# One transformer-trunk layer on one core: five 1024-column gate products as seven-product block sums, attention steps gathered among the transposed products

## The reference

```
h = rmsnorm(x, ln_g)
qa, ka, va, za, qb, ckv, iq, ik, iw, zb, qc, kc, vc, zc, ga, gb, gc = split(h @ w_in)   # 2048 rows deep
ya = mixer_a(qa, ka, va) * silu(za)       # window of two chunks, sinks, T5 bias
yb = mixer_b(qb, ckv, iq, ik, iw) * silu(zb)   # top-64 keys of an indexer, latent keys and values
yc = mixer_c(qc, kc, vc) * silu(zc)       # chunk-causal, relative bias
merged = sigmoid(ga) * (ya @ w_pa) + sigmoid(gb) * (yb @ w_pb) + sigmoid(gc) * (yc @ w_pc)
out = rmsnorm(x + merged @ w_o, final_g)
```

## Time and profile before

| | |
|---|---|
| median of three runs | 973.84 us |
| the profiled execution's own time | 973.51 us |
| its span, first to last instruction | 971.6 us |
| PE busy | 961.6 us (99%), 5114 matmuls |
| DVE busy | 608.5 us (63%) |
| ACT busy | 473.0 us (49%) |
| POOL busy | 28.2 us (3%) |
| DMA queues of SP | 56.9% of the 16 engines |
| granted PE clock | 0.997 of full speed |

### The profile page before, as it was taken

The page is one execution under the profiler, slowest core; times in us unless marked ns, Lnnn a source line. Parts: engine busy times, 40 slices in busy tenths (PEclk is TensorE's granted clock), DMA queues, the critical chain, the costliest instruction groups (busy, mean ns, idle before and its releaser), DMA issues.

```text
span 971.6 us, 13291 instructions
## 1 busy us (share of the span) xinstructions
PE 961.6 (99%) x5114; PEld 813.1 (84%) x5114; DVE 608.5 (63%) x1135; ACT 473.0 (49%) x786; POOL 28.2 (3%) x26
## 2 busy tenths in 40 slices
PE   9999999999999999999999999999999999999996
PEld 8788888888888888888888888888888888888885
DVE  7585755777675776586765655766655555555553
ACT  6564544555454545454453545544534443444442
POOL 0030000000000110010000000000000000000000
PEclk9999999999999999999999999999999999999998
DMA  8754755464653755564654745646555576555553
GB/s 342 274 194 130 244 200 187 151 225 162 207 205 120 253 174 180 189 207 157 222 199 139 261 157 178 227 149 216 167 193 179 191 304 221 186 184 187 174 177 126
DMA packets 54766, 190.34 MB, mean 196 GB/s; under 512 B 6192, under 2 KB 7088, under 8 KB 54064
## 3 DMA queue, kind: packets, MB, share of 16 engines
q1 hardware_dynamic: 54416, 189.23, 56.9%
q10 hardware_dynamic: 288, 0.27, 0.1%
HBM read 187.38 MB, written 2.10 MB: 195 GB/s over the span
## 4 chain that ended last, share of the span: by engine, by line
PE 94%; DVE 2%; DMA 2%; issue 1%; ACT 0%; SPq 0%; POOLq 0%; POOL 0%; DVEq 0%; ACTq 0%
PE bank L1025 23%; PE bank L1006 18%; PE bank L1008 18%; PE bank L1007 18%; PE bank L1028 12%; PE bank L981 2%; PE bank L1061 2%; PE bank L1081 2%; DMA raw<-in_w_s_dram 2%; DVE w_lo L626 1%; DVE hT L693 0%; ACT w_hi L444 0%; PE bank L1198 0%; DVE scores L686 0%; DVE denom L678 0%
## 5 line engine op out<-in xcount | busy, mean ns | idle before, releaser
L626 DVE TENSOR_TENSOR w_lo<-raw,w_hi 128x1024 fp32r<-128x1024 f32 (+2 forms) x326 | 387.2, 1211 | 172.8 <-ACT w_hi L444 171.4
L444 ACT ACTIVATE w_hi<-raw 128x1024 fp32r<-128x1024 f32 (+2 forms) x326 | 334.8, 1046 | 297.0 <-PE bank L1008 204.0
L1025 PE MATMUL bank<-hT,w_hi 128*128 128x512 f32 x976 | 306.2, 397 | 0.0
L1008 PE MATMUL bank<-w_hi,hT 128*128 128x512 f32 x568 | 221.1, 389 | 0.0
L1028 PEld LDWEIGHTS bank<-hT,w_lo 128*128 128x128 f32 x976 | 181.1, 188 | 41.1
L1006 PE MATMUL bank<-w_hi,hT 128*128 128x512 f32 x504 | 197.2, 391 | 0.0
L1007 PE MATMUL bank<-w_lo,hT 128*128 128x512 f32 x504 | 196.1, 389 | 0.0
L1028 PE MATMUL bank<-hT,w_lo 128*128 128x256 f32 x976 | 190.8, 278 | 0.0
L1025 PEld LDWEIGHTS bank<-hT,w_hi 128*128 128x128 f32 x976 | 150.6, 189 | 3.9
L1008 PEld LDWEIGHTS bank<-w_hi,hT 128*128 128x128 f32 x568 | 106.6, 188 | 22.3
L1006 PEld LDWEIGHTS bank<-w_hi,hT 128*128 128x128 f32 x504 | 94.6, 188 | 20.4 <-issue 0.2
(11 more groups left out here) (149 smaller groups left out, 559.6 us busy)
## 6 DMA issues: line engine op xcount, KB each, us to landing
raw<-in_w_s_dram SPq DMA_DIRECT2D x314, 512.0 KB, 4.4
bias_t<-in_bias_dram SPq DMA_DIRECT2D x24, 384.0 KB, 3.1
raw<-in_w_s_dram SPq DMA_DIRECT2D x6, 456.0 KB, 5.7
merged<-in_x_dram SPq DMA_DIRECT2D x2, 1024.0 KB, 10.5
raw<-in_w_s_dram SPq DMA_DIRECT2D x8, 256.0 KB, 3.1
big<-in_x_dram SPq DMA_DIRECT2D x1, 2048.0 KB, 9.8
out_dram<-big SPq DMA_DIRECT2D x8, 256.0 KB, 2.6
big<-in_x_t_dram SPq DMA_DIRECT2D x7, 256.0 KB, 5.9
```

The source lines that it names most:

```text
L444: nc.scalar.activation(halves(g)[0], raw[:, s, 0:n], ACT.Copy).then_inc(hi_ready, 1)
L626: nc.vector.tensor_tensor(low, raw[:, s, 0:n], high.bitcast(F32), ALU.subtract).then_inc(lo_ready, 1)
L1008: ins = mm(acc, xl, wh[:, e, :], start=False, stop=kt == n_kt - 1)
L1025: mm(bank[2 * (c % 2) + n][:, :], wh[:, e, n * P:(n + 1) * P], hl_t[:, kt, :, :], start=kt == 0, stop=False)
```

## The change

Five of the six gate parts of 1024 columns become one chunk of kind `G` (the first part, `ga`'s left half, stays as two `g` chunks). A `G` chunk takes the 2048-deep product as eight pairs of depth tiles, `k` and `k + 8`. In four of the eight pairs (`S` in `GROUPS`) the 2 x 2 block product (two halves of depth, two of rows; two of depth, two of columns) is formed with seven block products in place of eight. The other four pairs (`p`) are plain. An `S` pair has four pieces, whose block products are 2, 1, 2 and 2 (each is three matmuls of 512 columns); its first two come from DRAM, the last two are sums of weight blocks that POOL writes into `usum` (a ring of two). A `p` pair has two pieces of four block products.

ACT and DVE split the summed pieces like all others. The sums of activation blocks are made once, in chunks `g(0,0)` to `g(0,1)`. `G` accumulates in seven banks besides bank 7 for the plain part, so no attention may be under way: all 25 slots move ahead into the `q`, `k` and `z` chunks. There, slots up to 6 are five pieces apart and those behind alternate between five and two. The exponentials and the normalisation each come one step sooner after their scores. `z(0)` moves behind `k`, so attention output is now copied out by ACT unmultiplied (four copies a slot pair) and multiplied by `silu` at the end of each `z` chunk. The selection rounds of mixer B move from `z(0)` to the `q` chunks. `raw` gets six slots.

```diff
+GROUPS = "SpSpSpSp"
 def branch(b):
-    return [k for n in range(4) for k in (("g", b, n), ("P", b, n))]
+    first = [("g", b, 0), ("P", b, 0), ("g", b, 1), ("P", b, 1)]
+    return ((first if b == 0 else [("G", b, 0), ("P", b, 0), ("P", b, 1)])
+            + [("G", b, 1), ("P", b, 2), ("P", b, 3)])
+def group_pieces():
+    summed, plain = iter(range(NS)), iter(range(NS, 8))
+    return [(part, i) for k in GROUPS for i in [next(summed if k == "S" else plain)]
+            for part in (("11 22", "21 12", "U1 U3", "U2 U4") if k == "S" else ("p 11 22", "p 21 12"))]
...
-          + quarters("k", 0) + quarters("z", 1)
-          + branch(0) + quarters("z", 2) + branch(1) + branch(2) + quarters("o", 0))
+          + quarters("k", 0) + quarters("z", 0) + quarters("z", 1) + quarters("z", 2)
+          + branch(0) + branch(1) + branch(2) + quarters("o", 0))
+RAWS = 6
...
 def slots():
-    yield -1, FIRST[AT["z", 0, 3]]
-    whole = [g for g in range(FIRST[AT["q", 1, 0]], END["k", 0, 3]) if KIND_OF[g] in "qk"]
-    for i in range(8):
-        yield i, whole[2 + 6 * i]
-    for b in range(2):
-        yield 8 * b + 8, FIRST[AT["z", b + 1, 0]] + 2
-        for k in range(7):
-            yield 8 * b + 9 + k, FIRST[AT["g", b, 0]] + 2 + 6 * k
+    for i in range(-1, 7):
+        yield i, FIRST[AT["q", 1, 0]] + 2 + 5 * (i + 1)
+    for i in range(7, 24):
+        yield i, FIRST[AT["k", 0, 0]] + 6 + 7 * ((i - 7) // 2) + 5 * (i % 2 == 0)
...
             def load(g):
-                wait(sp, lo_ready, g - RING + 1)
+                if d >= RAWS:
+                    last = LOADED[d - RAWS]
+                    sp.wait_ge(lo_ready, last + 1)
+                    if last in PART and PART[last][2] in ("11 22", "21 12"):
+                        sp.wait_ge(u_sum, 3 * sum(k <= last + 2 for k in SUMS))
...
+            for n, g in enumerate(SUMS):
+                first, other = source(g - 2), raw[:, RAW_OF[g - 1] % RAWS, :]
+                u13, u24 = source(g), source(g + 1)
+                wait_source(pool, g - 2)
+                wait_source(pool, g - 1)
+                if n > 1:
+                    pool.wait_ge(lo_ready, SUMS[n - 2] + 2)
+                nc.gpsimd.tensor_tensor(two(u13), two(first),
+                                        other[:, CH:2 * CH].unsqueeze(1).to_broadcast([P, 2, CH]), ALU.add
+                                        ).then_inc(u_sum, 1)
+                pool.wait_ge(u_sum, 3 * n + 1)
+                nc.gpsimd.tensor_tensor(u24[:, 0:CH], u13[:, 0:CH], first[:, CH:2 * CH], ALU.add).then_inc(u_sum, 1)
+                pool.wait_ge(u_sum, 3 * n + 2)
+                nc.gpsimd.tensor_tensor(u24[:, CH:2 * CH], u24[:, 0:CH], other[:, 0:CH], ALU.add).then_inc(u_sum, 1)
...
             (ACT, attend)
+                    elif q >= 0:
+                        sc.wait_ge(pv_ready, q + 1)
+                        sc.wait_ge(scored, min(q + 2, NPAIR // 2))
+                        for p in (2 * q, 2 * q + 1):
+                            for t in range(NT):
+                                nc.scalar.activation(qT[p // 8][:, p % 8, P * t:P * (t + 1)],
+                                                     bank[4 + 2 * (p % 2) + t][:, SROW:CH], ACT.Copy, scale=0.25
+                                                     ).then_inc(o_ready, 1)
                 for e in range(2):
-                    p = scored_at(g - 3 - e) + e
+                    p = scored_at(g - 2 - e) + e
...
+            def tanh_sums(c):
+                for a in range(4):
+                    sc.wait_ge(g_final, 4 * sums_of(c) + a + 1)
+                    nc.scalar.activation(gx[:, a, :], gx[:, a, :], ACT.Tanh, scale=0.5).then_inc(tanh_ready, 1)
...
             (DVE, silu_chunk)
+                ve.wait_ge(o_ready, 4 * (4 * b + u + 1))
+                for half in range(2):
+                    m = 2 * u + half
+                    nc.vector.tensor_tensor(qT[b][:, m, :], qT[b][:, m, :], silu[:, half, :], ALU.mult
+                                            ).then_inc(y_ready, 1)
...
+            def finish_sums(c):
+                ve.wait_ge(used, FIRST[c + 1])
+                ve.wait_ge(g_comb, 4 * sums_of(c) + 4)
+                for a, n in enumerate((5, 4, 1, 7)):
+                    nc.vector.tensor_tensor(gx[:, a, :], gx[:, a, :], bank[n][:, :], ALU.add).then_inc(g_final, 1)
...
+            def block_product(n, left, w, half, start, stop):
+                wh, wl = (v[:, CH * half:CH * (half + 1)] for v in w)
+                mm(bank[n][:, :], left[0], wh, start=start, stop=False)
+                mm(bank[n][:, :], left[0], wl, start=False, stop=False)
+                return mm(bank[n][:, :], left[1], wh, start=False, stop=stop)
+            def group_step(g):
+                pe.wait_ge(lo_ready, g + 1)
+                if part == "11 22":
+                    block_product(2, block_of(i, 0, 0), w, 0, first, last)
+                    ins = block_product(4, sum_of(i, 1, 0), w, 1, first, False)
+                elif part == "21 12":
+                    ins = block_product(5, block_of(i, 1, 0), w, 0, first, False)
+                elif part == "U1 U3":
+                    block_product(6, sum_of(i, 1, 1), w, 0, first, last)
+                    if first:
+                        pe.wait_ge(dve_evac, dves_before(c))
+                    ins = block_product(0, sum_of(i, 0, 1), w, 1, first, last)
+                elif part == "U2 U4":
+                    block_product(3, sum_of(i, 0, 0), w, 0, first, last)
+                    ins = block_product(1, block_of(i, 1, 1), w, 1, first, False)
```

More of the change, by code:

```diff
@@ L52 @@
 END = {key: FIRST[c + 1] for key, c in AT.items()}
+PART = {FIRST[c] + j: (c, j, part, i) for c, k in enumerate(KINDS) if k == "G" for j, (part, i) in enumerate(GP)}
+SUMS = [g for g in range(NPIECE) if g in PART and PART[g][2] == "U1 U3"]
+LOADED = [g for g in range(NPIECE) if g not in PART or PART[g][2][0] != "U"]
+RAW_OF = {g: d for d, g in enumerate(LOADED)}
+N_G = KINDS.count("G")
 COPIED = ("kvc", "v", "uv")
@@ L98, in tanhs_before, with sums_of, base @@
 def tanhs_before(c):
-    return 2 * sum(k in "zg" for k in KINDS[:c])
+    return sum(4 if k == "G" else 2 * (k in "zg") for k in KINDS[:c])
+def sums_of(c):
+    return KINDS[:c].count("G")
+def base(c):
+    return 2 * ((c - sums_of(c)) % 2)
 def tanhs_z(c):
@@ new lines, in h_combine @@
+            def h_combine(n):
+                a11, a12, a21, a22 = (h_sum[:, :, k, t, :] for t in range(2) for k in range(2))
+                ve.wait_ge(h_summed, n + 2)
+                if n == 0:
+                    ins = nc.vector.tensor_tensor(a22, a21, a22, ALU.subtract)
+                elif n == 1:
+                    ins = nc.vector.tensor_tensor(a21, a11, a21, ALU.subtract)
+                elif n == 2:
+                    ins = nc.vector.tensor_tensor(a11, a22, a11, ALU.subtract)
+                else:
+                    ins = nc.vector.tensor_tensor(a12, a12, a11, ALU.add)
+                ins.then_inc(h_summed, 1)
```

238 lines of the change are left out of this document (178 added, 60 removed).

## The result

The changed kernel takes 1012.42 us (median of four runs, 1010.45 to 1015.27), the kernel before 973.97 us beside it: ratio 1.0402, 95% interval 1.0384 to 1.042. I had forecast 983 us and a range up to 992. The sign was right, the size was not: the loss is 38.5 us where I had worked out 9.

What follows compares the result with a forecast made beforehand. The kernel was taken to be bound by PE's number of matmuls, busy 99% of the span. 973.5 - 13.6 + 7.5 + 11 + 1 + 0.5 + 3 = 982.9, with 0.3 to the median 983 us; range 968 to 992.

Steps and rivals of the forecast that it cites:

- Matmuls: On PE, a `G` has 180 matmuls in place of 192; five of them save 13.6 us.
- Start of a `G`: Behind the merge, DVE's third-piece subtraction comes late: PE waits 1.75 us in four `G`, 0.5 in branch 0; 7.5 us.
- POOL's sums: POOL additions and DVE subtractions exclude each other; the third and fourth sums delay PE 2.2 us a `G`, 11 us.
- Splits of `y` and what lies behind a `G`: Further DVE work: two `y` splits in first `G` of branches 1 and 2, 1 us; additions behind a `G`, 0.5.
- Attention: Scores to normalised probabilities barely fit five pieces; mask additions or selection rounds make PE's transposes late, 3 us over twelve steps.
- A: Rival: POOL's additions fall into DVE's idle time or run ahead; 971, or 968 if attention costs nothing; chance 0.2.
- B: Rival: PE pays nothing, the start waits vanish too as DVE lets the third piece through sooner; 960; chance 0.04.
- C: Rival: attention becomes the bound, DVE falls behind in `z` chunks, each of twelve steps loses 1 us or more; 992; chance 0.15.
- D: Rival: accumulating in seven banks in turn slows the matmuls' pace; 1% slower would be 2 us; chance 0.03.
- The bound I gave for the sums: Upper bound for POOL's additions delaying PE: 49 us, if two sums of each `G` are paid in full.

Runs made afterwards that it cites:

- the fastest kernel: Changed kernel with weight sums and the eight mask additions on DVE instead of POOL, and a `G`'s third piece split ahead of the merge: 965.9 us, 0.9926.
- narrow sums: Changed kernel with each of POOL's three additions per `S` pair covering 8 columns in place of 1024 or 512: 976.48 us, 1.0034.
- after: The changed kernel itself, with the whole change against the kernel before: 1012.42 us, ratio 1.0402.
- Seven slots: Changed kernel with seven slots of `raw` in place of six, all POOL additions kept: 989.5 us, 1.0167.
- one-input copies: Changed kernel with POOL's three additions turned into copies of one input, of the same 1024, 512 and 512 columns: 979.96 us, 1.0065.
- first addition wide: Changed kernel with POOL's first addition at its full 1024 columns and the other two at 8: 983.55 us, 1.0103.
- two additions wide: Changed kernel with POOL's first two additions at full width and only the third at 8 columns: 1002.68 us, 1.0301.
- slow copies: Changed kernel with POOL's three additions replaced by one-input copies repeated two, three and three times: 991.5 us, 1.0184.
- attention alone: Changed kernel with all gates as `g` chunks of eight pieces, so no `G` and no sums; attention's new place kept: 977.71 us, 1.0045.

## Why the prediction was wrong

*Matmuls, -13.6:* right in pace, 0.227 us in a `G`. Of the 13.6 us the fastest kernel shows 7.3 in its time; 3.6 are lost in its five `G` (0.42 twice, 0.92 to 0.93 three times), 0.5 ahead of transposes, 2.2 I can't place. As much can come from the start alone: the profiled executions reach the 150th matmul at 36.95 to 39.14 us, and the two at the ends of that range are kernels that differ only in POOL's additions, which come later.

*Start of a `G`, 7.5:* right in mechanism, nearly in size. By itself it is 3 x 1.64 + 2 x 0.43 = 5.8 us of gaps (narrow sums). I counted four `G` behind a four-instruction merge, and there are three: the one that opens branch 1 comes behind branch 0's last merge, of two instructions.

*POOL's sums, 11:* this is the step that failed; it is 36 us (1012.42 - 976.48). Not through the durations: 2.4 + 1.3 + 1.3 = 5.0 us undisturbed against my 4.9. That the two exclude each other was right too. The placing itself, "the first sum is done ahead of the chunk and the second about as it starts", nearly held: the second starts 1.1 us into the `G`. What failed is the step from there, that these two cost nothing and only the third and fourth reach PE, at 2.2 us a `G`. Both early sums fall onto a merge. The spans of the two profiled executions, after and narrow sums, differ by 37.9 us, and the start times place them:

- 11.9 us at the start of the three `G` behind a four-instruction merge (5.72 + 5.35 + 5.76 against 3 x 1.64). The second sum falls on that merge, where DVE is already the last one due.
- 4.2 us by a slow PE behind these gaps (below). I had no such term.
- 5.4 us between two `P` chunks, where the first sum lies on the other merge. I had nothing there.
- 17.2 us inside the `G`, the starts of the first two among it: 3.8 and 5.5 us in these, 2.4 to 2.8 in the other three, against my 2.2. This part is nearest to what I had worked out.
- 0.9 us less ahead of the first `G`.

I laid out one addition, where three come in a row and DVE is let in once between two of them. Seven slots, with the same sums at other moments, take 23 of the 36 us away.

The slow PE, in windows (stretch and its length, busy us of PE, PEld, DVE, ACT, POOL, then the granted clock, the DMA share and GB/s):
```profile
841.30:843.40 2.10, 2.10 (x10) 1.50 (x8) 1.91 (x3) 1.53 (x2) 0.97 (x1) 1.00 0.89 298
849.20:852.20 3.00, 2.91 (x7) 2.33 (x8) 3.00 (x4) 0.00 (x0) 0.00 (x0) 0.50 0.00 0
852.20:856.00 3.80, 3.80 (x18) 3.15 (x17) 2.27 (x3) 1.69 (x2) 0.00 (x0) 0.98 0.81 258
```
Behind 5.76 us of idleness the clock stands at 0.50 (1.2 GHz) for 3 us: seven steps from one matmul to the next take 3.10 us instead of 1.59. That is 1.5 us lost, and the two others lose 1.5 and 1.7. Behind a gap of narrow sums the steps lose 0.2 us, so the slow clock costs 4.2 us in the three.

How much of DVE's held time reaches PE: the first number is what the groups `w_lo` (1024 columns of `raw`, of `usum`, and 512 columns) and `merged` have over those with narrow sums (349.5, 48.5, 19.1 and 10.3 us), the second the median over that kernel's.

| kernel | DVE held, us | PE pays, us |
|---|---|---|
| one-input copies | 11.9 | 3.5 |
| first addition wide | 19.1 | 7.1 |
| seven slots | 35.1 | 13.0 |
| two additions wide | 40.7 | 26.2 |
| slow copies | 50.5 | 15.0 |
| after | 69.5 | 35.9 |

A microsecond held costs PE 0.3 to 0.6 us, and more of them need not cost more: the slow copies hold DVE longer than two wide additions and cost little more than half as much. I read this as a matter of where they fall.

*Splits of `y` and what lies behind a `G`, 1.5:* too small to be told apart; no gap shows there in the narrow-sum kernel. *Attention, 3:* attention alone is +4.7 us, of which 3.0 are PE's gaps. I had the mask additions as one of three causes; moving them to DVE takes the gaps to 0.5 us and the time from 969.75 to 965.9, so they are most of it. In the profiled executions 0.8 us of the difference lie ahead of the 150th matmul, where both kernels do the same.

*Rivals.* A (sums hidden) didn't happen: even with seven slots the sums cost 13 us. B (nothing paid) is disproved by 5.8 us of start gaps. C is not what happened: the time is beyond its 992, but attention's gaps are 3 us, not 12. D (a slower pace) isn't there. The bound I gave for the sums, 49 us, held the value; my range left it out, since I trusted a placing of four sums worked out.

*What stays open:* how the 36 us divide exactly between held instructions of DVE and late sums. The repeated copies change both. That ACT waits only 1.9 us for sums in after speaks for the held instructions, and so does that with narrow sums it waits 10.0 us for them and PE shows no gap for it.
